# The second feed-forward's down-projection with tokens on partitions, and the last norm, residual and output in token rows

## What is computed

```python
def conv_glu(x, w_gate_up, conv_ffn, w_down):
    gu = x @ w_gate_up
    gate, up = jnp.split(gu, 2, axis=-1)
    gate = causal_dwconv_2(gate, conv_ffn)
    return (jax.nn.silu(gate) * up) @ w_down

def rmsnorm(x, g):
    xf = x.astype(jnp.float32)
    y = xf * lax.rsqrt(jnp.mean(xf * xf, axis=-1, keepdims=True) + RMS_EPS)
    return (y * g.astype(jnp.float32)).astype(x.dtype)
...
        f = conv_glu(rmsnorm(h, g_pre_ffn), w_gate_up, conv_ffn, w_down)
        h = h + rmsnorm(f, g_post_ffn)
    return h[:, N_META:]
```

## Time and profile before

| | us |
|---|---|
| runs | 2725.75, 2725.69, 2718.6 (median 2725.69) |
| the profiled execution, its own time | 2717.22 |
| its span, first to last instruction | 2715.5 |
| PE busy in the span | 2553.2 (94%) |
| DVE busy | 1720.3 (63%) |
| ACT busy | 1183.2 (44%) |
| POOL busy | 130.2 (5%) |
| mean granted PE clock | 0.968 of full speed |

### The profile page before, as it was taken

How to read it: one execution, slowest core, us unless ns; L and a number is a source line. 1 busy time by engine, 2 the same in 40 slices (tenths; PEclk the granted TensorE clock), 3 DMA queues, 4 the chain that set the end, 5 groups by cost and what they waited for, 6 DMA issues and landing times.

```text
span 2715.5 us, 62451 instructions
## 1 busy us (share of the span) xinstructions
PE 2553.2 (94%) x26109; PEld 2480.1 (91%) x26109; DVE 1720.3 (63%) x2183; ACT 1183.2 (44%) x1377; POOL 130.2 (5%) x132
## 2 busy tenths in 40 slices
PE   7999877999999999999899999998899999999996
PEld 7899856999999999999789888987899999999996
DVE  6675665766666666668665555555666666666666
ACT  4344533444444444445533342333444444444442
POOL 1000000100000000002100000002300000000003
PEclk8999977999999999999999999999899999999998
DMA  5555322555555555555433333335355555555552
GB/s 186 151 167 162 118 89 67 186 186 183 184 184 185 184 185 185 185 170 167 147 90 108 101 99 101 103 117 171 117 183 182 183 180 184 179 185 179 184 170 85
DMA packets 419354, 419.27 MB, mean 154 GB/s; under 512 B 15310, under 2 KB 417474, under 8 KB 418946
## 3 DMA queue, kind: packets, MB, share of 16 engines
q1 hardware_dynamic: 418722, 415.41, 49.8%
q10 hardware_dynamic: 496, 1.84, 0.2%
HBM read 415.10 MB, written 2.10 MB: 154 GB/s over the span
## 4 chain that ended last, share of the span: by engine, by line
PE 83%; DVE 9%; ACT 3%; PEld 2%; issue 1%; POOL 1%; DMA 0%; ACTq 0%; SPq 0%; DVEq 0%; POOLq 0%; PEldq 0%
PE psum L2015 26%; PE psum L2016 25%; PE psum L2017 25%; PE psum L2336 3%; DVE w_lo L1072 2%; ACT w_hi L645 1%; DVE head_r L1184 1%; DVE mixed L1971 1%; PEld psum L2017 1%; PEld psum L2015 1%; PEld psum L2016 1%; PE psum L2506 1%; DVE act_lo L1110 1%; DVE up L1091 0%; DVE conv_out L1281 0%
## 5 line engine op out<-in xcount | busy, mean ns | idle before, releaser
L2015 PE MATMUL psum<-act_hi,w_hi 128*128 128x256 f32 (+4 forms) x4880 | 1410.2, 289 | 74.6 <-DVE act_lo L1110 16.9
L2016 PE MATMUL psum<-act_lo,w_hi 128*128 128x256 f32 (+4 forms) x4880 | 1385.8, 284 | 0.0
L2017 PE MATMUL psum<-act_hi,w_lo 128*128 128x256 f32 (+4 forms) x4880 | 1382.1, 283 | 3.1 <-issue 3.1
L645 ACT ACTIVATE w_hi<-raw 128x1024 fp32r<-128x1024 f32 x788 | 828.2, 1058 | 1097.5 <-PE psum L2017 1067.4
L1072 DVE TENSOR_TENSOR w_lo<-raw,w_hi 128x1024 fp32r<-128x1024 f32 x788 | 958.3, 1230 | 506.9 <-ACT w_hi L645 506.4
L2015 PEld LDWEIGHTS psum<-act_hi,w_hi 128*128 128x128 f32 (+1 forms) x4880 | 930.3, 191 | 95.3 <-issue 38.3
L2017 PEld LDWEIGHTS psum<-act_hi,w_lo 128*128 128x128 f32 (+1 forms) x4880 | 931.3, 191 | 2.9 <-issue 2.9
L2016 PEld LDWEIGHTS psum<-act_lo,w_hi 128*128 128x128 f32 (+1 forms) x4880 | 931.5, 191 | 2.2 <-issue 1.2
L2015 PE MATMUL psum<-ff_hi,w_hi 128*128 128x256 f32 x1280 | 363.7, 284 | 13.4 <-DVE up L1091 6.5
L2016 PE MATMUL psum<-ff_lo,w_hi 128*128 128x256 f32 x1280 | 361.5, 282 | 0.0
L2017 PE MATMUL psum<-ff_hi,w_lo 128*128 128x256 f32 x1280 | 361.3, 282 | 0.0
(11 more groups left out here) (338 smaller groups left out, 1545.5 us busy)
## 6 DMA issues: line engine op xcount, KB each, us to landing
raw<-in_w_in SPq DMA_DIRECT2D x188, 512.0 KB, 4.0
raw<-in_w_up SPq DMA_DIRECT2D x176, 512.0 KB, 3.6
raw<-in_w_down SPq DMA_DIRECT2D x176, 512.0 KB, 4.5
raw<-in_w_gate_up SPq DMA_DIRECT2D x176, 512.0 KB, 3.6
raw<-in_w_out SPq DMA_DIRECT2D x64, 512.0 KB, 4.6
x_rows<-in_x SPq DMA_DIRECT2D x2, 1024.0 KB, 6.1
out_x<-out_rows SPq DMA_DIRECT2D x8, 256.0 KB, 2.5
raw<-in_w_in SPq DMA_DIRECT2D x4, 384.0 KB, 3.4
```

Of the source, the lines that this page charges most:

```text
L645: act.activation(w_hi[:, slot], raw[:, slot], ACT.Copy).then_inc(S["hi_done"], 1)
L2015: pe.matmul(out_, wh, xh, start=first and r == 0, stop=False)
L2016: pe.matmul(out_, wh, xl, start=False, stop=False)
L2017: mm = pe.matmul(out_, wl, xh, start=False, stop=last and r == RK - 1)
```

## The change

In the second feed-forward, `downs` uses a new `rows_unit`. The tile of activations (128 features x 128 tokens, `ff_hi` or `ff_lo`) is the stationary operand, and 512 columns of weights are the moving one. A unit now holds 2 blocks of 128 rows x 512 columns rather than 4 x 256, and has 12 matmuls of 512 columns rather than 24 of 256. Two units make a group (4 groups in a chunk rather than 8), and a group's two banks hold 512 output features of tokens 0 to 127 and 128 to 255. The first feed-forward and all up-projections stay as they are.

The accumulator is `f_rows`, the memory of `mixed` seen as 2 x 2048 columns with tokens on partitions. POOL clears it rather than DVE. The weights of the last norm come as a broadcast DMA of 1 MB into `g_rows` (the memory of `squares2`) on SP's queue. The residual is turned into token rows ahead of the last `downs` (32 transposes, L2375 of the changed kernel) and copied by ACT to `out_rows`. At the end ACT squares the token rows of each group with a sum along the row, DVE multiplies by `g_rows`, the 1/rms is made for one number per token, and 8 DVE instructions (scale and add) write `out_rows`. The ones-matmul, the 16 `post`, the 16 adds of POOL and the 8 PSUM copies of DVE behind the last matmul are gone.

```diff
-    stream.phase("ffn2", 4 * FCH + 8 * FCH, 24 * FCH)
+    stream.phase("ffn2", 4 * FCH + 4 * FCH, 24 * FCH)
...
+    f_rows = M["mixed"][:].rearrange("p k t -> p (k t)")[:, 0:2 * D] \
+        .rearrange("p (b n) -> p b n", b=2)
+    g_rows = M["squares2"][:].rearrange("p k t -> p (k t)")[:, 0:D]
...
@@ SyncE: loads @@
+            def rows_load(u, slot, src):
+                sp.wait_ge(S["lo_done"], u - NSLOT + 1)
+                dst = raw[:, slot].rearrange("p (r n) -> p r n", r=2)
+                sp.dma_start(dst, src).then_inc(landed[slot], 16)
...
                 ups(u, 0)
+                if by_rows:
+                    sp.wait_ge(*norm_at("n4", "add", 5))
+                    sp.dma_start(g_rows, g_post_ffn_2.unsqueeze(0).to_broadcast([P, D])) \
+                        .then_inc(S["g_rows_landed"], 16)
...
@@ GpSimd @@
-            sum_squares("n5", M["squares2"], T1)
-            add_post(KD, TC1, False)
+            pool.wait_ge(S["post"], KD)
+            pool.memset(f_rows, 0.0).then_inc(S["f_cleared"], 1)
...
@@ ScalarE, end of ffn2 @@
+            def rows_end(w, g):
+                act.activation(M["row_ss"][:, 0, 7:8], ones[:, 0:1], ACT.Sqrt) \
+                    .then_inc(S["row_root"], 1)
+                for n in range(8):
+                    gg, tt = divmod(n, 2)
+                    act.wait_ge(S["h_turned"], n + 1)
+                    act.activation(M["out_rows"][:, tt, 512 * gg:512 * gg + 512],
+                                   psum[:, 4 + n % 4], ACT.Copy).then_inc(S["h_copied"], 1)
+                for n in range(8):
+                    gg, tt = divmod(n, 2)
+                    if n in (0, 2):
+                        hi(w + n, n)
+                        hi(w + n + 1, n + 1)
+                    act.wait_ge(S["last_left"], n + 1)
...
+                    act.activation(sq_rows[:, n % 4], f_rows[:, tt, 512 * gg:512 * gg + 512],
+                                   ACT.Square, accum_out=M["row_ss"][:, tt, gg:gg + 1]) \
+                        .then_inc(S["f_squared"], 1)
+                act.wait_ge(S["row_inv"], 1)
+                act.activation(M["row_ss"][:, :, 6], M["row_ss"][:, :, 6], ACT.Sqrt) \
+                    .then_inc(S["row_root"], 1)
...
@@ VectorE, evictions in ffn2 @@
+                def leave_rows(v, g):
+                    leave(v + 2 * g + 2, (pair0 + g) % 2, f_rows[:, :, 512 * g:512 * g + 512], 512,
+                          how="added")
+
+                def downs_leave(v, d):
+
+                    if not by_rows:
+                        leave_down(v, d)
+                        lo(v + 4 + d, d % 4)
+                    else:
+                        lo(v + 4 + d, d % 4)
+                        if d % 2 == 0:
+                            leave_rows(v, d // 2)
...
@@ VectorE, end of ffn2 @@
+                for g in range(4):
...
+                    dve.wait_ge(S["unit_used"], w + 10 + 2 * g)
+                    for tt in range(2):
+                        dve.tensor_tensor(f_rows[:, tt, cs], psum[:, 2 * ((pair0 + g) % 2) + tt],
+                                          f_rows[:, tt, cs], ALU.add).then_inc(S["last_left"], 1)
...
+                    if g < 3:
+                        dve.wait_ge(S["f_squared"], 2 * g + 2)
+                        dve.tensor_tensor(f_rows[:, :, cs], f_rows[:, :, cs],
+                                          over(g_rows[:, cs], 1, 2), ALU.mult) \
+                            .then_inc(S["f_weighted"], 1)
+                    else:
+                        dve.wait_ge(S["last_left"], 8)
+                        dve.tensor_tensor(fg_last, f_rows[:, :, cs], over(g_rows[:, cs], 1, 2),
+                                          ALU.mult).then_inc(S["f_weighted"], 1)
+                dve.wait_ge(S["f_squared"], 8)
+                link(dve.tensor_reduce(ss[:, :, 4], ss[:, :, 0:4], AX_X, ALU.add))
+                link(dve.tensor_scalar(ss[:, :, 5], ss[:, :, 4], 1.0 / D, EPS, ALU.mult, ALU.add))
+                dve.reciprocal(ss[:, :, 6], ss[:, :, 5]).then_inc(S["row_inv"], 1)
...
+                for n in range(8):
...
+                    dve.scalar_tensor_tensor(out=M["out_rows"][:, tt, cs], in0=fg,
+                                             scalar=ss[:, tt, 6:7], in1=M["out_rows"][:, tt, cs],
+                                             op0=ALU.mult, op1=ALU.add) \
+                        .then_inc(S["out_copied"], 1)
...
-            dve.wait_ge(S["post"], KD)
-            link(dve.memset(mixed[:], 0.0))
-            ffn("ffn2", "n4", LEAD, c_gconv, False, mixed, lambda d: None)
-            rstd_of("n5", T1, D, EPS)
-            for k in range(KD):
-                post(c_postffn, TC1, k)
...
@@ TensorE @@
+            def rows_unit(u, slot, pair, hi_, lo_, k0, first, last):
+
+                pe.wait_ge(S["lo_done"], u + 1)
+                for r in range(2):
+                    wh = w_hi[:, slot, 512 * r:512 * r + 512]
+                    wl = w_lo[:, slot, 512 * r:512 * r + 512]
+                    for b in range(2):
+                        out_, t = psum[:, 2 * pair + b], slice(P * b, P * b + P)
+                        xh, xl = hi_[:, k0 + r, t], lo_[:, k0 + r, t]
+                        pe.matmul(out_, xh, wh, start=first and r == 0, stop=False)
+                        pe.matmul(out_, xh, wl, start=False, stop=False)
+                        mm = pe.matmul(out_, xl, wh, start=False, stop=last and r == 1)
+                mm.then_inc(S["unit_used"], 1)
...
+                if by_rows:
+                    for n in range(8):
+                        c, tt = divmod(n, 2)
+                        if n >= 4:
+                            pe.wait_ge(S["h_copied"], n - 3)
+                        for k in range(4):
+                            mm = pe.transpose(psum[:, 4 + n % 4, P * k:P * k + P],
+                                              resid[:, 4 * c + k, T0 + P * tt:T0 + P * tt + P],
+                                              ident[:])
+                        mm.then_inc(S["h_turned"], 1)
```

More of the change, by code:

```diff
@@ L1476, in ffn @@
                 leave_up(u, 3)
+                if by_rows:
+                    dve.wait_ge(S["f_cleared"], 1)
                 with dve.Fori(1, FCH - 1) as i:
@@ L1497, in ffn, with norm_on @@
                         product_lo(i, M["last_hi"], M["last_lo"])
+                ending(w, pair0, leave_down)
+            def norm_on(w, pair0, leave_down):
                 for d in range(8):
                     leave_down(w + 8, d)
[L1500 to L1506, removed]
+                    lo(w + 12 + d, d % 4)
+                    norm_pair("n2", c_premix, TC2, d - 1)
@@ L1508, in _ @@
+            ffn("ffn1", "n1", 0, c_fconv, True, False, norm_on)
             norm_pair("n2", c_premix, TC2, 7)
@@ L1982, in _ @@
                     norm_lo("n4", c_preffn, TC3, (k - 3,))
-            dve.wait_ge(S["post"], KD)
-            link(dve.memset(mixed[:], 0.0))
-            ffn("ffn2", "n4", LEAD, c_gconv, False, mixed, lambda d: None)
-            rstd_of("n5", T1, D, EPS)
-            dve.wait_ge(S["evicted"], stream.groups)
-            for k in range(KD):
-                post(c_postffn, TC1, k)
-            for n in range(8):
-                g, tt = divmod(n, 2)
-                dve.wait_ge(S["out_turned"], n + 1)
-                dve.tensor_copy(M["out_rows"][:, tt, 512 * g:512 * g + 512], psum[:, 4 + n % 4]) \
-                    .then_inc(S["out_copied"], 1)
+            ffn("ffn2", "n4", LEAD, c_gconv, False, True, rows_end)
         @block.tensor
@@ L2250, in downs @@
                     pe.wait_ge(S["ff_fflo"], i + (n0 + 1))
+                    if by_rows:
+                        for d in range(8):
+                            n, k = divmod(d, 2)
+                            if k == 0 and (not isinstance(i, int) or n < 2):
+                                bank_free(g + n)
+                            elif k == 0:
+                                pe.wait_ge(S["last_left"], 2 * n - 2)
+                            rows_unit(v + d, d % 4, (pair0 + n) % 2, hi_, lo_, 2 * k, k == 0,
+                                      k == 1)
+                        return
                     for d in range(8):
@@ L2570, in _ @@
             sum_over("n3", T3)
-            ffn("ffn2", "n4", T3, TC3)
-            sum_over("n5", T1)
-            for n in range(8):
-                g, tt = divmod(n, 2)
-                if n == 3:
-                    pe.wait_ge(*norm_at("n5", "ms", 1))
-                if n >= 4:
-                    pe.wait_ge(S["out_copied"], n - 3)
-                pe.wait_ge(S["post"], KD + 4 * g + 4)
-                for k in range(4):
-                    mm = pe.transpose(psum[:, 4 + n % 4, P * k:P * k + P],
-                                      resid[:, 4 * g + k, T0 + P * tt:T0 + P * tt + P], ident[:])
-                mm.then_inc(S["out_turned"], 1)
+            ffn("ffn2", "n4", T3, TC3, True)
 _INS = [
```

81 lines of the change are left out of this document (50 added, 31 removed).

## The result

The changed kernel takes 2689.6 us (median of 4 runs, 2688.1 to 2692.3), the kernel before 2722.1 beside it (4 runs). The ratio is 0.9896, with a 95% interval from 0.9883 to 0.991: 1.0% faster. The profiled execution's span falls from 2715.5 to 2687.4 us, by 28.1, where the prediction's sum had 33.3. Windows of the kernel after, in the columns of the earlier trace rows: a steady chunk's downs, chunk 9's, the transposes, the last downs (to the start of their last matmul), the tail.

The account below looks back on a forecast made before the run. The prediction took the kernel as PE-bound (chain of waits 83% PE). Its terms summed to -33.3 us, taking the profiled 2717.2 to 2684; with the 8.5 us offset 2692, stated as 2691, range 2685 to 2697.

Parts of the forecast that it names:

- nine steady downs: Downs of chunks 0 to 8, second feed-forward: 21.75 instead of 23.3 us each, -14.0 us in all.
- downs of chunk 9: Second feed-forward's chunk 9: 22.1 us instead of 27.4, with no clock loss, -5.3 us.
- transposes: Moved from behind the last matmul to ahead of the last downs, with PE partly idle: +5.5 us.
- fall of the clock: One fall of PE to 1.2 GHz after its partial idleness at the transposes: +1.6 us, bounds 0 and 3.2.
- tail: From the last matmul to the end of the span: 12.0 instead of 31.4 us, -19.4 us.
- start: DVE's 3.69 us clearing goes to POOL, so PE's wait for the split behind it goes: -0.7 us.
- Matmuls of 512 columns: In the downs, the surplus is a fixed part, so 512 columns take 225 ns against 234.6 for two of 256.
- the first rival: In the downs, the surplus grows with the columns: 234.6 ns per matmul, 10.1 us more, 2701 us; chance 0.14.
- starts of groups: In each steady chunk's downs they cost little; 0.15 us was kept for them.
- the stall goes: PE's 0.4 us stall per steady chunk on the late up eviction vanishes; the group needing it starts 5.4 us later.
- The walk over DVE: DVE's work in chunk 9's downs, step by step: second eviction ends at 16.6 us, PE waits 0.4 us for it.
- The 1 MB of `g_rows`: Load on SP's queue between the loads of chunks 0 and 1: 0 us, bound +3.

Follow-up runs that it names:

- the edit of the kernel before: Kernel before, with DVE's fourth up eviction put ahead of its fourth weight split in the second feed-forward; 2707.7 us, ratio 0.9972 to the kernel before.

## Why the prediction was right, and where it was off

All stages are cut from start to start of matmuls, the last downs at the end of their last matmul.

| term | forecast | measured (spans) |
|---|---|---|
| nine steady downs | -14.0 | -8.0 (23.30 to 22.40 each) |
| ups between them | | +0.1 |
| downs of chunk 9 | -5.3 | -4.9 |
| last downs | -1.05 | -0.2 |
| transposes | +5.5 | +5.25 |
| fall of the clock | +1.6 | 0 |
| tail | -19.4 | -19.8 |
| start | -0.7 | -0.9 |
| upstream, untouched | | +0.6 |
| sum | -33.3 | -28.0 |

The forecast time was met, and four of the seven terms hold to 0.4 us, but the first one, the largest gain in PE's stream, didn't come from the cause that it names.

**Matmuls of 512 columns** is the term that was mis-sized. "A fixed part, not one that grows clearly with the columns" was false: the part grows with the columns (10 ns at 256, 20 at 512). That is the mechanism of the first rival, which had a chance of 0.14. Two points of a line, 256 and 272, were both taken with tokens moving, where the place of the operand alone shifts the pitch by more than the 0.9 ns between the two surpluses; and the plain passes, taken as a sign of a small fixed part, read a column every two cycles and so never meet the limit. 8.4 ns x 1056 is 8.9 us over the forecast.

Some of it came back, and by luck. The forecast kept 0.15 us a chunk for starts of groups, but there is no gap at all in these downs; and no fall of the clock followed PE's idle 1.47 us. Last, the executions shown on record before ran 8.5 us above the profiled one, which the median of after did by 0.4 only. So the time came out at 2690 by errors of both signs: the offset of 8.5 us, which has nothing to do with the change, about cancels the 8.9. Without it the forecast would have been 2684, just under its own range of 2685 to 2697.

Where the gain of the downs did come from: 0.57 us of a chunk's 0.90 by the removed stall (the prediction's step "the stall goes", shown by the edit of the kernel before), 0.31 by the operand that moves (116.7 against 118.3 ns), none by the width. Of chunk 9's gain, too, that edit alone gave 3.2 us in the kernel before (27.35 to 24.12).

**Chunk 9.** The walk over DVE had the second down eviction 0.4 us late. It was in time, and PE ran through. The walk itself was good: the eviction ended 16.3 us after the start of these downs, against 16.6. But a unit took 2.8 us rather than 2.7, so that the seventh was needed at 16.8 and not at 16.2. **The transposes** and **the tail** hold to 0.3 and 0.4 us, with the mechanism named: the table load and ACT's first copy for the one; for the other the short steps (four in the chain, 0.75 us, where the sum had five and 1.05) and 8 row instructions of some 0.67 us. **The 1 MB of `g_rows`** cost nothing: no PE wait stands in chunks 0 and 1.

## What to carry to other kernels

Take the rate of a matmul from a row with the same moving operand, and at two widths that lie far apart, before calling a surplus fixed: 256 and 272 columns could not tell 225 from 234 ns, 256, 384 and 512 could. Here the read of the moving operand sets a rate, and an instruction of 512 columns rather than 256 doesn't help it. A restructuring may gain by what it reorders, so try the reordering alone: here one eviction ahead of one split gives 0.57 us a chunk in either feed-forward, and transposes that stand in a norm's waits are free, where in the stream they cost their full length.

## What was not expected of the hardware

fp32r matmuls at 2.4 GHz are held to some 2.2 moving columns a ns (116.7 ns for 256, 176.6 for 384, 233.4 for 512), at 1.2 GHz they run one column a cycle (427 ns for 512), and with one repeated column one a cycle at the full clock (215.8). PEld busy 100% or 80% of the time makes no difference to it (downs of 22.41 and 22.40 us).

Beside POOL's sums of squares a split of weights on DVE takes up to 2.75 us instead of 1.21, beside POOL's clearing it takes 1.21: four of them take 7.8 us in after and 4.6 in before, where DVE's own clearing keeps them clear of the sums.

PE's wait of 2.28 us in chunk 9 of before was followed by a fall of the clock; waits of 1.47 us (after) and 1.14 us (the edit of before) were not.
